# Second-layer weights in pieces of two depth blocks by all columns, instead of whole depth by 256 columns

## The chip, the cores and the metric

The kernel runs on one core of one Trainium2 chip. The metric is the device time of one execution in microseconds (us). A measurement is the median of several runs.

## What is computed

A two-layer decoder trunk on 256 positions of width 1024, in float32. Layer 0 is a gated short convolution, layer 1 a forgetting attention whose key, value and forget gates come from the residual stream. Both layers also attend to 256 memory rows, and both end in a PEER layer: 128 table rows per position are chosen out of 16,384, and gathered from two tables.

```python
for layer in range(2):
    if layer == 1:
        hs = rmsnorm(x, g_kv)
        zkv = hs @ w_kv                     # keys 768, values 768, forget gates 12 columns
    h = rmsnorm(x, g_mix[layer])
    mkv = rmsnorm(mem, g_mem[layer]) @ w_mem_kv[layer]
    if layer == 0:
        z = h @ w_in_a[0]                   # u, c, b (768 each), memory queries 256
        y_main = b_gate * causal_dwconv(c_gate * u, conv_w[0])
    else:
        z = h @ w_in_b[0]                   # queries 768, memory queries 256
        y_main = fox_attention(qf, k_sh, v_sh, logf_sh)
    x = x + concatenate([y_main, mem_attention(qm, mk, mv)]) @ w_out[layer]
    # peer: q = xn @ w_q; top 16 x 16 keys per head, 8 heads; then for each position
    #   a = xn . u_tab[idx];  w = softmax(score) * gelu(a);  out = sum(w * v_tab[idx])
    x = x + peer(rmsnorm(x, g_ffn[layer]), peer_wq[layer], ...)
return rmsnorm(x, g_final)
```

## The kernel before

**Phases and groups.** The positions are cut into two chunks of 128, one position per partition. A phase is one chunk's PEER layer: phases 0 and 1 are layer 0 of chunks 0 and 1, phases 2 and 3 are layer 1 (chunk c has phase c + 2). A phase has 16 groups, and a group handles 8 of the 128 table rows of each position. Each of the 8 slots of a group takes one gather of 128 u rows and one of 128 v rows, 4 KB per row, into `u_ring` and `v_ring` (8 slots each). GpSimd issues them (`fetch`, line 519; `group`, line 536): the v gather of slot s waits until the sums of the group before have read that slot, the u gather of the next group until VectorE's dot product of that slot is done. VectorE makes the dots (line 1010) and folds in one v slot itself (line 1037); ScalarE makes gelu, gates and seven diagonal matrices (lines 596 to 611); TensorE adds the other seven v slots into PSUM `acc` (line 795).

**Side steps.** The rest of the network is cut into steps, and `make_schedule` (line 71) writes out by hand in which group each is done: `SIDE[phase, group]`. TensorE does the side steps of a group ahead of that group's sums; VectorE and ScalarE do them after that group's dots and diagonals. A route step (`("route", ph, h)`) projects one head's 256 query columns, transposes them, scores them against the keys on TensorE, and gives VectorE the choice of the top rows. VectorE runs that part (line 1258) spread between the dots of the next group, in order. The attention, key, value, query and output steps of layer 1 of chunk c lie in groups 0 to 9 of phase c + 1: keys in group 1, values and forget gates in 2, queries in 3, attention in 4 to 8, output in 8.

**Weights.** SyncE loads all weights in pieces of 1 MB in the order of their first use (line 468). A piece is the whole depth (8 blocks of 128 rows) by 256 columns, so each run in memory is 1 KB. Eight pieces of the first layer have places of their own inside the gather rings (`HELD`), one lies in `kv_buf` (`GUEST`), all others take turns in `w_ring` with `NW` = 5 slots. A load into a slot waits for the last tile that uses the piece five places earlier (line 480), and SyncE keeps its order. The `out` and `q` pieces of layer 0 are loaded once for both chunks, those of layer 1 once for each chunk.

**Tiles.** A projection's result is a PSUM tile in one of four banks (six at the start). Keys and queries are made with the weights as the stationary side (`columns_out`, line 768: two blocks of 128 columns in a tile), values, outputs and routes with the activations stationary (`tokens_out`, line 777: 256 columns in a tile). `take` (line 747) waits for the bank, `piece_landed` (line 415) for the piece, `filled` and `emptied` (lines 396 and 399) for a tile. The first output tile of a chunk waits for all parts of `yT` (line 868).

Of the kernel before, what the change touches and what calls it, by code (L numbers as in the profile page):

```python
# [32 lines left out]
P = 128  # L33
# [8 lines left out]
CONV_K = 3  # L42
PC = 256
NPAIR = D // P
HEADS = 8
# [25 lines left out]
def make_schedule():  # L71

    def attn(ph, *ks):
        return [("attn", ph, k) for k in ks]

    def out(ph, *cols):
        return [("out", ph, i) for i in cols]

    def conv(c, *parts):
        return [("in", c, int(p[1]), p[0]) for p in parts]

    def rms(*step):
        return ("rms", step)


    chunk0 = [*conv(0, "b0"), ("mem_k", 0), *conv(0, "u1"), ("in_q",), ("mem_v", 0), *attn(0, 0), *conv(0, "c1"),
              *attn(0, 1), *conv(0, "b1"), *attn(0, 2), *conv(0, "u2"), *attn(0, 3), *conv(0, "c2"), ("keys", 0),
              *conv(0, "b2"), *out(0, 0, 1, 2, 3)]  # L90
# [118 lines left out]

def piece_of(tile):  # L210

    kind = tile[0]
    if kind == "mT":
        return "mem", tile[1]
    if kind == "key":
        return "keys", tile[1]
    if kind == "out":
        return (kind, 0, tile[2]) if tile[1] < 2 else tile
    if kind == "q":
        return (kind, 0, tile[2]) if tile[1] < 2 else tile  # L220
    if kind in ("u", "c", "b"):
        return kind, tile[2]
    return tile if kind in ("mk", "mv", "qm", "k", "v", "qf") else None

# [3 lines left out]
for _t in TILES:  # L228
    if piece_of(_t):
        LAST_USE[piece_of(_t)] = _t  # L230

# [5 lines left out]
for _n in range(NW, len(PIECES)):  # L237
    assert TILE[LAST_USE[PIECES[_n - NW]]] < min(TILE[t] for t in TILES if piece_of(t) == PIECES[_n])


def trunk(nc, x, mem, g_mix, w_in_a, conv_w, w_in_b, w_out, g_mem, w_mem_kv, g_kv, w_kv, b_f, g_ffn,
# [5 lines left out]
    def weight_source(key):  # L247
# [4 lines left out]
        if kind == "keys":  # L252
            return peer_keys[key[1]].rearrange("h t n d -> n (h t) d")
        w, col = {
            "mk": lambda: (w_mem_kv[key[1]], 0),
# [4 lines left out]
            "qm": lambda: (w_in_a[0], 3 * CONV),  # L260
            "k": lambda: (w_kv, PC * key[2]),
            "v": lambda: (w_kv, CONV + PC * key[2]),
            "qf": lambda: (w_in_b[0], PC * key[2]),
            "out": lambda: (w_out[key[1] // 2], PC * key[2]),
            "q": lambda: (peer_wq[key[1] // 2], PC * key[2]),
# [3 lines left out]
    with ExitStack() as ctx:  # L269
# [186 lines left out]
        def _(sp):  # L456
# [11 lines left out]
            for key in LAST_USE:  # L468
                src = weight_source(key)
                dst = piece(key).rearrange("p (a b) -> p a b", a=src.shape[1])  # L470
                if key in HELD:
# [9 lines left out]
                sp.dma_start(dst, src).then_inc(w_landed[n % NW], 16)  # L481
                if key == ("out", 0, 0):
                    load_gain_row(g_ffn[0])
# [104 lines left out]
        def _(act):  # L588
# [32 lines left out]
            def side(step):  # L621
# [24 lines left out]
                elif kind == "k":  # L646
                    _, c, i = step
                    if c == 0 and i == 0:
                        filled(act, ("mv", 1))
                    copy_tile(step, kT[:, 2 * i:2 * i + 2, P * c:P * c + P],  # L650
                              bank(step)[:, 0:2 * P].rearrange("p (a b) -> p a b", a=2))
                elif kind == "v":
                    _, c, i = step
                    copy_tile(step, vals[:, c, PC * i:PC * i + PC], bank(step)[:, 0:PC])
                elif kind == "forget":
                    act.wait_ge(fabs_made, step[1] + 1)
                    act.activation(fz[:, 2, :], fz[:, 1, :], ACT.Exp, scale=-1.0).then_inc(fexp_made, 1)
                elif kind == "qf":
                    _, c, i = step
                    if c == 1:  # L660
                        filled(act, ("lg", 2, NPAIR - 1))
                    copy_tile(step, qT[:, 2 * i:2 * i + 2, :],
                              bank(step)[:, 0:2 * P].rearrange("p (a b) -> p a b", a=2))
                elif kind == "attn":
# [30 lines left out]
                    if k >= 2:  # L695
                        key = ("y", ph, k - 2)
                        if ph >= 2 and k == 2:
                            filled(act, ("out", ph - 2, 3))
                        copy_tile(key, yT[:, pairs[k - 2], P * c:P * c + P], bank(key)[:, 0:P])
# [44 lines left out]
        def _(pe):  # L744
# [32 lines left out]
            def tokens_out(key, src):  # L777
# [4 lines left out]
                done(project(t[:, 0:PC], src, lambda k: w[:, k, :]))  # L782

            def transposes(key, blocks):
                t = take(key)
# [14 lines left out]
            def side(step):  # L800
# [44 lines left out]
                elif kind == "k":  # L845
                    if step[2] == 0:
                        for i in range(2):
                            emptied(pe, ("nT", step[1], i))
                    columns_out(step, lambda k: hT[:, k, 0:P], P)
                elif kind == "v":  # L850
                    tokens_out(step, lambda k: hT[:, k, 0:P])
                elif kind == "forget":
# [9 lines left out]
                elif kind == "qf":  # L862
                    columns_out(step, lambda k: hT[:, k, P:2 * P], P)
# [37 lines left out]
            def attention(ph, k):  # L901

                c, pairs = ph % 2, attention_pairs(ph)
                if k == 0:
                    if ph < 2:
                        emptied(pe, ("qm",))
                    else:
                        for i in range(4):
                            emptied(pe, ("qf", c, i))
                        for i in range(3):  # L910
                            emptied(pe, ("k", c, i))
# [69 lines left out]
        def _(dve):  # L981
# [102 lines left out]
            def start_norm(step):  # L1084
# [11 lines left out]
                elif kind == "ffn":  # L1096
                    ph = step[1]
                    if ph >= 2:
                        filled(dve, ("fT", ph - 2, 1))
                    for i in range(4):  # L1100
                        emptied(dve, ("out", ph, i))
# [7 lines left out]
            def side(step):  # L1109
# [22 lines left out]
                elif kind == "norm":  # L1132
                    c = step[1]
                    filled(dve, ("qf", 0, 3) if c else ("b", 1, NB // 2 - 1))
                    for i in range(2):
# [11 lines left out]
                elif kind == "out":  # L1147
                    _, ph, i = step
                    filled(dve, step)
                    part = xres[:, ph % 2, PC * i:PC * i + PC]  # L1150
                    empties(dve.tensor_tensor(part, part, bank(step)[:, 0:PC], ALU.add), step)
                elif kind == "ffn":
# [249 lines left out]
```

## Time and profile before

| | |
|---|---|
| Runs | 1630.38 us median of 3 (1630.02 to 1630.99) |
| Profiled execution | span of 1628.2 us from the first to the last instruction; its own total is not given apart from the span |
| TensorE busy | 1330.9 us, 82% |
| VectorE busy | 1073.0 us, 66% |
| ScalarE busy | 468.4 us, 29% |
| GpSimd busy | 1013.0 us, 62% |
| DMA | 619.20 MB, mean 380 GB/s |
| Mean granted TensorE clock | 0.907 of full speed |

A busy share is an average over stages that have different limits. The page cuts the span into 40 slices, each of 40.7 us. The first three slices are the start (first layer up to the first routes), and the gathers run from 117 us to the end. On the DMA lines q0 is GpSimd's queue of gathers, and q1 SyncE's queue of weights and other plain loads. Every gather is reported with some very small packets beside its 4 KB ones.

### The profile page before, as it was taken

The page shows a single profiled execution, that of the slowest core. Times are in us where ns is not written, and L with a number is a line of the kernel's source. Part 1 is how long each engine was busy: PE and PEld are TensorE (multiplying, and loading weights), DVE is VectorE, ACT ScalarE, POOL GpSimd, SP SyncE. Part 2 cuts the span into 40 slices and gives each one's busy share as a digit, 9 for nine tenths or more (in the row PEclk, how much of TensorE's full clock was granted, in tenths as well). Part 3 has the DMA queues.
Part 4 walks back from the last instruction along what each step waited for, and adds up shares of the span by engine and source line. Part 5 has one row for each costly group of instructions (what it writes and reads, how often), then busy time and mean ns, then how long its engine had stood idle before and what let it go on. Part 6 is the DMA issues. An engine that isn't in the chain of part 4 may idle for free.

```text
span 1628.2 us, 17186 instructions
## 1 busy us (share of the span) xinstructions
PE 1330.9 (82%) x4558; PEld 768.0 (47%) x4558; DVE 1073.0 (66%) x2529; ACT 468.4 (29%) x1427; POOL 1013.0 (62%) x1099
## 2 busy tenths in 40 slices
PE   7999789888885899887877789989868877777775
PEld 7887544444552564354444366545434432222222
DVE  4248689988775445638778835674878985555555
ACT  0203343333332222433233222451333321111112
POOL 0006677777547656667666654675776777777764
PEclk9999898999998999899888899999999988888887
DMA  9519999999999999999999999999999999999997
GB/s 336 185 53 372 397 399 409 405 404 405 379 391 378 396 393 394 409 405 390 401 401 403 401 376 384 397 397 393 400 403 409 409 411 409 410 409 410 410 409 272
DMA packets 224232, 619.20 MB, mean 380 GB/s; under 512 B 18914, under 2 KB 90652, under 8 KB 224156
## 3 DMA queue, kind: packets, MB, share of 16 engines
q0 software_dynamic: 147456, 536.94, 83.7%
q1 hardware_dynamic: 76699, 81.36, 15.0%
q8 instruction: 35, 0.57, 0.1%
q14 instruction: 42, 0.34, 0.1%
HBM read 617.17 MB, written 1.05 MB: 380 GB/s over the span
## 4 chain that ended last, share of the span: by engine, by line
PE 36%; DMA 22%; POOL 13%; issue 12%; DVE 9%; ACT 5%; POOLq 0%; SPq 0%; DVEq 0%; ACTq 0%
DMA u_ring<-in_peer_u_dram,idx_now 20%; PE acc L795 18%; PE tile L765 13%; POOL u_ring L520 7%; POOL v_ring L520 7%; DVE u_ring L1010 4%; ACT diag L610 2%; DMA v_ring<-in_peer_v_dram,idx_now 2%; ACT gelus L604 2%; PE xf L765 1%; PE tile L897 1%; PE tile L924 1%; PE tile L892 1%; PE tile L928 0%; PE tile L787 0%
## 5 line engine op out<-in xcount | busy, mean ns | idle before, releaser
L795 PE MATMUL acc<-v_ring,diag 128*128 128x512 f32 x1780 | 852.9, 637 | 118.5 <-ACT diag L610 74.0
L1010 DVE CUSTOM_DVE_ANT_0 u_ring<-u_ring,xf 128x1024 f32<-128x1024 f32 x512 | 613.2, 1216 | 270.2 <-DMA u_ring<-in_peer_u_dram,idx_now 267.2
L520 POOL DMA_INDIRECT v_ring<-in_peer_v_dram,idx_now x512 | 495.4, 968 | 294.5 <-issue 121.9
L795 PEld LDWEIGHTS acc<-v_ring,diag 128*128 128x128 f32 x1780 | 359.9, 207 | 581.3 <-issue 565.9
L520 POOL DMA_INDIRECT u_ring<-in_peer_u_dram,idx_now x512 | 503.3, 983 | 173.4 <-issue 126.5
L596 ACT ACTIVATE gelus<-dots 128x8 f32<-128x8 f32 x64 | 13.4, 209 | 515.4 <-DVE dots L1010 515.4
L610 ACT ACTIVATE diag<-ident,gelus 128x128 f32<-128x128 f32 x448 | 137.8, 388 | 2.1
L765 PE MATMUL tile<-w_ring,fT 128*128 128x256 f32 x480 | 110.4, 384 | 6.4 <-DVE fT L1159 6.4
L765 PEld LDWEIGHTS tile<-w_ring,fT 128*128 128x128 f32 x480 | 92.0, 192 | 30.3 <-issue 12.0
L604 ACT ACTIVATE gelus<-gelus,gates 128x1 f32<-128x1 f32 x512 | 102.1, 281 | 4.9 <-ACT gelus L596 3.3
L714 ACT ACTIVATE gexp<-best,gstat 128x16 f32<-128x16 f32 x32 | 9.8, 307 | 306.9 <-DVE best L1300 306.9
L892 PE MATMUL tile<-ident,q_rows 128*128 128x128 f32 x64 | 17.7, 368 | 86.7 <-ACT q_rows L704 86.7
L1037 DVE SCALAR_TENSOR_TENSOR xres<-v_ring,gelus,xres 128x1024 f32<-128x1024 f32 x63 | 80.9, 1284 | 8.7 <-issue 8.7
L765 PE MATMUL tile<-hT,w_ring 128*128 128x128 f32 (+1 forms) x544 | 69.7, 293 | 15.1 <-issue 13.1
L765 PEld LDWEIGHTS tile<-hT,w_ring 128*128 128x128 f32 x544 | 68.0, 203 | 17.7 <-issue 14.5
L570 POOL COPY idx_now<-idx_all 128x8 uint32<-128x8 uint32 x1 | 0.2, 187 | 114.2 <-DVE idx_all L1329 114.2
L596 ACT ACT_TABLE_LOAD x45 | 57.7, 1283 | 0.8
L765 PE MATMUL tile<-w_ring,yT 128*128 128x256 f32 x224 | 51.1, 389 | 5.8 <-ACT yT L619 4.9
L892 PEld LDWEIGHTS tile<-ident,q_rows 128*128 128x128 f32 x64 | 7.7, 169 | 99.6 <-ACT q_rows L704 99.6
L765 PEld LDWEIGHTS tile<-w_ring,yT 128*128 128x128 f32 x224 | 43.3, 195 | 12.5 <-issue 6.4
L897 PE MATMUL tile<-keysT,pq 128*128 128x128 f32 x128 | 32.4, 396 | 15.1 <-ACT pq L706 15.1
L1010 DVE DVE_READ_ACCUMULATOR2_ANT dots<- 128x1 f32 x512 | 42.1, 82 | 0.0
(170 smaller groups left out, 1043.0 us busy)
## 6 DMA issues: line engine op xcount, KB each, us to landing
w_ring<-in_peer_wq_dram SPq DMA_DIRECT2D x23, 1024.0 KB, 16.5
w_ring<-in_w_out_dram SPq DMA_DIRECT2D x12, 1024.0 KB, 16.8
w_ring<-in_w_kv_dram SPq DMA_DIRECT2D x12, 1024.0 KB, 16.9
u_ring<-in_peer_u_dram,idx_now POOLq DMA_INDIRECT x512, 11.5
v_ring<-in_peer_v_dram,idx_now POOLq DMA_INDIRECT x512, 11.0
w_ring<-in_w_in_b_dram SPq DMA_DIRECT2D x8, 1024.0 KB, 16.5
u_ring<-in_w_in_a_dram SPq DMA_DIRECT2D x4, 1024.0 KB, 12.2
w_ring<-in_w_mem_kv_dram SPq DMA_DIRECT2D x4, 1024.0 KB, 15.4
```

The source lines that it names most:

```text
L520: pool.indirect_dma_start(ring[:, s, :], None, rows_[:, :], bass.IndirectOffsetOnAxis(idx_now[:, column + s:column + s + 1], 0), element_o ...
L596: act.activation(gelus[:, par * G:par * G + G], dots[:, par * G:par * G + G], ACT.Gelu)\
L604: act.activation(gelus[:, par * G + s:par * G + s + 1], gelus[:, par * G + s:par * G + s + 1], ACT.Copy, scale=gate[:, col + s:col + s + 1 ...
L610: act.activation(diag[:, par * G + s, :], ident[:, :], ACT.Copy, scale=gelus[:, par * G + s:par * G + s + 1]).then_inc(diag_made, 1)
L714: act.activation(gexp[:, :], best[:, :], ACT.Exp, bias=gstat[:, 0:1], accum_out=gstat[:, 1:2]).then_inc(gexp_made, 1)
L765: ins = pe.matmul(out_ap, lhs(k), rhs(k), start=(k == 0), stop=(k == KD - 1))
L795: ins = pe.matmul(acc[:, 512 * n:512 * n + 512], diag[:, par * G + s, :], v_ring[:, s, 512 * n:512 * n + 512], start=(first and s == 0), s ...
L892: ins = pe.transpose(t[:, P * a:P * a + P], q_rows[:, P * a:P * a + P], ident[:, :])
L897: ins = pe.matmul(t[:, NKEY * a:NKEY * a + NKEY], pq[:, a, :], keysT[:, 2 * h + a, :], start=True, stop=True)
L924: ins = pe.matmul(t[:, hh, 0:width], q, keys, start=True, stop=not fox)
L1010: dve.tensor_tensor_reduce(u_ring[:, s, :], u_ring[:, s, :], xf[:, :], 1.0, 0.0, ALU.mult, ALU.add, dots[:, par * G + s:par * G + s + 1])\
L1037: dve.scalar_tensor_tensor(out=row, in0=v_ring[:, s, :], scalar=gelus[:, par * G + s:par * G + s + 1], in1=row, op0=ALU.mult, op1=ALU.add) ...
```

## The change

The second layer's key, value and query weights, and the output weights of both layers, are cut the other way: a piece holds two depth blocks (256 rows) by all wanted columns. Key and value pieces have 768 columns, 3 KB rows and 0.79 MB; query and output pieces have 1024 columns, 4 KB rows and 1.05 MB. Four pieces make one matrix, and every tile reads all four (`pieces_of`). The tiles become wider to fit: keys in tiles of 4 and 2 blocks, queries in two tiles of 4 blocks, values in two tiles of 384 columns, outputs in two of 512. Value and output tiles wait for their pieces two blocks at a time, and the first output tile waits for the parts of `yT` as it comes to them; key and query tiles wait for all four pieces at once. The step `("route", 0, 2)` moves from the head of the side steps of group (0, 1) to their end. The pieces of routes, memory and the other first-layer weights stay as they are.

```diff
+VC = CONV // 2
+OC = D // 2
+K_BLOCKS = [4, 2]
...
-    side[0, 0] += [*conv(1, "c2", "b2"), ("route", 0, 1), *out(1, 0, 1)]
-    side[0, 1] += [*out(1, 2, 3), rms("ffn", 1)]
+    side[0, 0] += [*conv(1, "c2", "b2"), ("route", 0, 1), *out(1, 0)]
+    side[0, 1] += [*out(1, 1), rms("ffn", 1)]
...
-    side[0, 1][0:0] = [("route", 0, 2)]
+    side[0, 1] += [("route", 0, 2)]
...
-        mix[1] += [("norm", c), ("k", c, 0), ("k", c, 1), ("k", c, 2)]
-        mix[2] += [("v", c, 0), ("v", c, 1), ("v", c, 2), ("forget", c)]
-        mix[3] += [("qf", c, 0), ("qf", c, 1), ("qf", c, 2), ("qf", c, 3)]
+        mix[1] += [("norm", c), ("k", c, 0), ("k", c, 1)]
+        mix[2] += [("v", c, 0), ("v", c, 1), ("forget", c)]
+        mix[3] += [("qf", c, 0), ("qf", c, 1)]
...
-        mix[8] += attn(ph, 9) + out(ph, 0, 1, 2, 3) + [rms("ffn", ph)]
+        mix[8] += attn(ph, 9) + out(ph, 0, 1) + [rms("ffn", ph)]
...
-def piece_of(tile):
+def pieces_of(tile):
...
+    if kind in ("k", "v", "qf"):
+        return [("w" + kind, tile[1], kk) for kk in range(KD // 2)]
     if kind == "out":
-        return (kind, 0, tile[2]) if tile[1] < 2 else tile
+        return [("wout", max(tile[1] - 1, 0), kk) for kk in range(KD // 2)]
...
+        if kind in ("wk", "wv", "wqf", "wout"):
+            w, col, width = {
+                "wk": lambda: (w_kv, 0, CONV),
+                "wv": lambda: (w_kv, CONV, CONV),
+                "wqf": lambda: (w_in_b[0], 0, D),
+                "wout": lambda: (w_out[min(key[1], 1)], 0, D),
+            }[kind]()
+            k = 2 * key[2]
+            return w.rearrange("(k p) n -> p k n", p=P)[:, k:k + 2, col:col + width]
...
+            def blocks_out(key, src, blocks, width):
+
+                t = take(key)
+                for at in pieces_of(key):
+                    piece_landed(pe, at)
+                for a, b in enumerate(blocks):
+                    ins = project(t[:, P * a:P * a + P], lambda k: rows_of(key, k, P * b, width), src)
+                done(ins)
+
+            def tokens_wide(key, src, cols, width, order=range(KD), ready=None):
+
+                t = take(key)
+                for n, k in enumerate(order):
+                    if n % 2 == 0:
+                        piece_landed(pe, pieces_of(key)[k // 2])
+                        if ready:
+                            ready(k // 2)
+                    ins = pe.matmul(t[:, 0:len(cols)], src(k), rows_of(key, k, None, width)[:, cols.start:cols.stop],
+                                    start=(n == 0), stop=(n == KD - 1))
+                done(ins)
...
-                    if i == 0:
-                        for k in range(len(attention_pairs(ph))):
-                            emptied(pe, ("y", ph, k))
-                        if ph < 2:
-                            for j in range(NB // 2):
-                                emptied(pe, ("b", ph, j))
-                    tokens_out(step, lambda k: yT[:, k, P * (ph % 2):P * (ph % 2) + P])
+                    order = [6, 7, 0, 1, 2, 3, 4, 5] if ph < 2 else range(KD)
...
+                    tokens_wide(step, lambda k: yT[:, k, P * (ph % 2):P * (ph % 2) + P],
+                                range(OC * i, OC * i + OC), D, order, mixed if i == 0 else None)
```

## Rows read from the trace of the kernel before

**Rows 1.** The page: DMA share and rate in 40 slices, and the weight queue.
```profile
DMA  9519999999999999999999999999999999999997
GB/s 336 185 53 372 397 399 409 405 404 405 379 391 378 396 393 394 409 405 390 401 401 403 401 376 384 397 397 393 400 403 409 409 411 409 410 409 410 410 409 272
...
q1 hardware_dynamic: 76699, 81.36, 15.0%
```

**Rows 2.** Busy time by stretch; last columns: TensorE clock, DMA share, GB/s.
```profile
551.00:596.00 45.00, 41.06 (x158) 26.28 (x157) 18.80 (x44) 11.16 (x36) 21.27 (x24) 0.92 1.05 386
650.00:700.00 50.00, 36.95 (x108) 17.03 (x107) 32.32 (x64) 25.42 (x83) 35.47 (x37) 0.87 1.03 409
```

**Rows 3.** Waits over the span: waiting, releaser, us in total, times, longest.
```profile
DVE u_ring L1010 <- DMA u_ring<-in_peer_u_dram,idx_now: 267.2, 218, 5.7
```

**Rows 4.** DMA queues, 551 to 596 us: packets, MB, share of 16 engines.
```profile
q1 hardware_dynamic: 6001, 6.06, 40.8%
```

**Rows 5.** DMA queues, 156 to 158 us.
```profile
q1 hardware_dynamic: 696, 0.70, 110.1%
```

**Rows 6.** DMA queues, 186 to 192 us.
```profile
q0 software_dynamic: 339, 1.26, 52.9%
q1 hardware_dynamic: 349, 1.17, 49.1%
```

**Rows 7.** Timeline of TensorE, 163 to 201 us: start, duration, instructions, idle before.
```profile
163.81 3.62 PE L765 MATMUL tile<-w_ring,fT 128*128 128x256 f32 x16
167.92 0.44 PE L892 MATMUL tile<-ident,q_rows 128*128 128x128 f32 x2 [0.49 <-ACT q_rows L704]
...
169.38 7.07 PE L765 MATMUL tile<-w_ring,yT 128*128 128x256 f32 x32
176.28 12.18 PE L795 MATMUL acc<-v_ring,diag 128*128 128x512 f32 x28
...
200.17 0.69 PE L892 MATMUL tile<-ident,q_rows 128*128 128x128 f32 x2 [7.37 <-ACT q_rows L704]
```

**Rows 8.** DMA queues at 150 to 152 us, and the weight issue at 148.
```profile
q1 hardware_dynamic: 1, 0.00, 0.1%
...
w_ring<-in_peer_wq_dram SPq DMA_DIRECT2D x1, 1024.0 KB, 9.9
```

**Rows 9.** Timeline of GpSimd, 153 to 206 us.
```profile
153.48 0.19 POOL L550 COPY idx_now<-idx_all 128x8 uint32<-128x8 uint32 x1 [3.67 <-DVE idx_all L1329]
153.95 0.96 POOL L520 DMA_INDIRECT v_ring<-in_peer_v_dram,idx_now  x1 [0.28 <-PE acc L795]
...
178.44 0.96 POOL L520 DMA_INDIRECT v_ring<-in_peer_v_dram,idx_now  x1 [4.00 <-PE acc L795]
...
206.03 0.96 POOL L520 DMA_INDIRECT v_ring<-in_peer_v_dram,idx_now  x1 [4.91 <-PE acc L795]
```

**Rows 10.** Timeline of VectorE: the first instruction of route (0, 2).
```profile
182.57 0.49 DVE L1266 MAX8 topv<-tile 128x8 f32<-128x128 f32 x2
```

**Rows 11.** Timeline of TensorE, 555 to 612 us.
```profile
555.19 12.18 PE L795 MATMUL acc<-v_ring,diag 128*128 128x512 f32 x28
567.21 10.52 PE L765 MATMUL tile<-w_ring,hT 128*128 128x256 f32 x48
...
597.82 14.45 PE L765 MATMUL tile<-hT,w_ring 128*128 128x128 f32 x128
```

**Rows 12.** Timeline of GpSimd: the gathers that end its two stalls.
```profile
557.89 0.96 POOL L520 DMA_INDIRECT v_ring<-in_peer_v_dram,idx_now  x1 [7.18 <-DVE dots L1010]
...
957.29 0.96 POOL L520 DMA_INDIRECT v_ring<-in_peer_v_dram,idx_now  x1 [12.71 <-PE acc L795]
```

**Rows 13.** DMA queues, 950 to 958 us.
```profile
q1 hardware_dynamic: 2374, 2.40, 91.9%
```

**Rows 14.** Timeline of TensorE: the output steps of chunks 0 and 1, layer 1.
```profile
716.61 14.05 PE L765 MATMUL tile<-w_ring,yT 128*128 128x256 f32 x64 [1.35 <-ACT yT L619]
...
1115.49 15.74 PE L765 MATMUL tile<-w_ring,yT 128*128 128x256 f32 x64 [3.59 <-ACT yT L619]
```

More of the change, by code:

```diff
@@ L89, in make_schedule @@
               *attn(0, 1), *conv(0, "b1"), *attn(0, 2), *conv(0, "u2"), *attn(0, 3), *conv(0, "c2"), ("keys", 0),
-              *conv(0, "b2"), *out(0, 0, 1, 2, 3)]
+              *conv(0, "b2"), *out(0, 0, 1)]
     chunk1 = [*conv(1, "b0", "u1", "c1"), *attn(1, 0), *conv(1, "b1"), *attn(1, 1), *conv(1, "u2"), *attn(1, 2, 3)]
@@ L207, with piece_of @@
 LAST_ROUTE = {ph: [r for r in ROUTES if r[0] == ph][-1] for ph in range(PHASES)}
-def piece_of(tile):
+def pieces_of(tile):
     kind = tile[0]
     if kind == "mT":
-        return "mem", tile[1]
+        return [("mem", tile[1])]
     if kind == "key":
-        return "keys", tile[1]
+        return [("keys", tile[1])]
+    if kind in ("k", "v", "qf"):
+        return [("w" + kind, tile[1], kk) for kk in range(KD // 2)]
     if kind == "out":
-        return (kind, 0, tile[2]) if tile[1] < 2 else tile
+        return [("wout", max(tile[1] - 1, 0), kk) for kk in range(KD // 2)]
     if kind == "q":
-        return (kind, 0, tile[2]) if tile[1] < 2 else tile
+        return [(kind, 0, tile[2]) if tile[1] < 2 else tile]
     if kind in ("u", "c", "b"):
-        return kind, tile[2]
-    return tile if kind in ("mk", "mv", "qm", "k", "v", "qf") else None
+        return [(kind, tile[2])]
+    return [tile] if kind in ("mk", "mv", "qm") else []
+def piece_of(tile):
+    return pieces_of(tile)[0]
 LAST_USE = {}
 for _t in TILES:
-    if piece_of(_t):
-        LAST_USE[piece_of(_t)] = _t
+    for _p in pieces_of(_t):
+        LAST_USE[_p] = _t
 HELD = [("c", 0), ("b", 0), ("u", 1), ("c", 1), ("b", 1), ("u", 2), ("c", 2), ("b", 2)]
@@ L237 @@
 for _n in range(NW, len(PIECES)):
-    assert TILE[LAST_USE[PIECES[_n - NW]]] < min(TILE[t] for t in TILES if piece_of(t) == PIECES[_n])
+    assert TILE[LAST_USE[PIECES[_n - NW]]] < min(TILE[t] for t in TILES if PIECES[_n] in pieces_of(t))
 def trunk(nc, x, mem, g_mix, w_in_a, conv_w, w_in_b, w_out, g_mem, w_mem_kv, g_kv, w_kv, b_f, g_ffn,
@@ L260, in weight_source @@
             "qm": lambda: (w_in_a[0], 3 * CONV),
[L261 to L264, printed above, removed]
             "q": lambda: (peer_wq[key[1] // 2], PC * key[2]),
@@ L469, in _ @@
                 src = weight_source(key)
-                dst = piece(key).rearrange("p (a b) -> p a b", a=src.shape[1])
+                dst = piece(key)[:, 0:src.shape[1] * src.shape[2]].rearrange("p (a b) -> p a b", a=src.shape[1])
                 if key in HELD:
@@ L481, in _ @@
                 sp.dma_start(dst, src).then_inc(w_landed[n % NW], 16)
-                if key == ("out", 0, 0):
+                if key == ("wout", 0, 0):
                     load_gain_row(g_ffn[0])
@@ L661, in side @@
                         filled(act, ("lg", 2, NPAIR - 1))
-                    copy_tile(step, qT[:, 2 * i:2 * i + 2, :],
-                              bank(step)[:, 0:2 * P].rearrange("p (a b) -> p a b", a=2))
+                    copy_tile(step, qT[:, 4 * i:4 * i + 4, :],
+                              bank(step)[:, :].rearrange("p (a b) -> p a b", a=4))
                 elif kind == "attn":
@@ L697, in side @@
                         if ph >= 2 and k == 2:
-                            filled(act, ("out", ph - 2, 3))
+                            filled(act, ("out", ph - 2, 1))
                         copy_tile(key, yT[:, pairs[k - 2], P * c:P * c + P], bank(key)[:, 0:P])
@@ L782, in tokens_out, with rows_of @@
                 done(project(t[:, 0:PC], src, lambda k: w[:, k, :]))
+            def rows_of(key, k, first, width):
+                at = pieces_of(key)[k // 2]
+                w = piece(at)[:, 0:2 * width].rearrange("p (k n) -> p k n", k=2)
+                return w[:, k % 2, first:first + P] if first is not None else w[:, k % 2, :]
+            def blocks_out(key, src, blocks, width):
[15 more added lines that the diff above has]
+                done(ins)
             def transposes(key, blocks):
@@ L848, in side @@
                             emptied(pe, ("nT", step[1], i))
-                    columns_out(step, lambda k: hT[:, k, 0:P], P)
+                    i = step[2]
+                    blocks_out(step, lambda k: hT[:, k, 0:P], range(4 * i, 4 * i + K_BLOCKS[i]), CONV)
                 elif kind == "v":
-                    tokens_out(step, lambda k: hT[:, k, 0:P])
+                    i = step[2]
+                    tokens_wide(step, lambda k: hT[:, k, 0:P], range(VC * i, VC * i + VC), CONV)
                 elif kind == "forget":
@@ L862, in side @@
                 elif kind == "qf":
-                    columns_out(step, lambda k: hT[:, k, P:2 * P], P)
+                    blocks_out(step, lambda k: hT[:, k, P:2 * P], range(4 * step[2], 4 * step[2] + 4), D)
                 elif kind == "attn":
@@ L907, in attention @@
                     else:
-                        for i in range(4):
+                        for i in range(2):
                             emptied(pe, ("qf", c, i))
-                        for i in range(3):
                             emptied(pe, ("k", c, i))
@@ L1099, in start_norm @@
                         filled(dve, ("fT", ph - 2, 1))
-                    for i in range(4):
+                    for i in range(2):
                         emptied(dve, ("out", ph, i))
@@ L1133, in side @@
                     c = step[1]
[L1134 removed]
+                    filled(dve, ("qf", 0, 1) if c else ("b", 1, NB // 2 - 1))
                     for i in range(2):
@@ L1149, in side @@
                     filled(dve, step)
-                    part = xres[:, ph % 2, PC * i:PC * i + PC]
-                    empties(dve.tensor_tensor(part, part, bank(step)[:, 0:PC], ALU.add), step)
+                    part = xres[:, ph % 2, OC * i:OC * i + OC]
+                    empties(dve.tensor_tensor(part, part, bank(step)[:, 0:OC], ALU.add), step)
                 elif kind == "ffn":
```

13 lines of the change are left out of this document (10 added, 3 removed).

## The prediction

> **What bounds the kernel now.** Read the page first: the DMA engines are over nine tenths busy in every slice but the first three, at 370 to 411 GB/s [rows 1]. A stretch of gathers alone moves 409 GB/s at a share of 1.03, the full rate [rows 2]. The waits agree: VectorE waits 267.2 us for rows of the u table, 218 times, never over 5.7 us [rows 3], a steady drip as behind a full queue. So from the first gather to the end the time is the DMA work divided by its rate, plus whatever idle DMA time a stall makes. The change touches both.
>
> **The work, smaller.** With both queues loaded, 551 to 596 us, the rate is 386 GB/s against 409 [rows 2]: 45 us x 23/409 = 2.53 us lost, on 6.06 MB of weights [rows 4], that is 0.44 us for a piece of 1.05 MB. The packets say why: weights alone, 696 packets of 1 KB took 110.1% of 16 engines for 2 us, 50.6 ns each, 50 us of engine time a MB [rows 5]. In the one stretch where the weight queue holds 4 KB rows (mem and the gain row, 186 to 192 us) it moved 1.17 MB in 49.1% of 96 us, 40.3 us a MB, and the gathers beside it 1.26 MB in 52.9%, the same [rows 6]. So 4 KB rows should give the 0.44 us back, and 3 KB rows, by a fixed cost per packet, 8/9 of it, 0.39 us. Twelve MB of key and value weights and sixteen of query and output weights in the two streaming chunks: 12 x 0.39 + 16 x 0.44 = 11.7 us. Bounds: nothing, and 28 x 0.53 = 14.8 us by the engine shares instead of the rate. I take the rate, since in a mix the share reads 1.05 and part of it is overlap [rows 2]. The first layer's output weights load before any gather: nothing.
>
> Against this stands a rule of the Trainium skill (DMA: Bandwidth & Descriptors, Specifications): line rate needs only transfers of 512 B or more, by which 1 KB rows lose nothing and this term is zero. By that rule, the 50 and 40 us a MB should have been equal; the trace disagrees.
>
> **Work on the engines.** Columns and passes stay; the matmuls are wider and fewer. Two 256-column output tiles take 7.07 us [rows 7], and a group of seven 2 x 512-column sums 12.18 us, 0.87 us for 512 columns against 0.44 for 256: no gain. Copies and adds of twice the width lie beside other work: nothing. The output step of the first chunk no longer waits for the last gate product before its first matmul: -0.6 us (0 to -0.9), as that start is a chain.
>
> **The moved step, route 2 of the first chunk.** All four first-layer output pieces are now last used by output tile 1 of chunk 1, in group 1. The query piece (0, 2) takes the slot of the first, so it can load only then; and TensorE's very next step is the route that needs it. Before, it was issued at 148.54 and landed 9.9 us later [rows 8], under the first group's sums. Now TensorE starts at 163.81 with the output tile (7.07 us) and is done at 170.9 [rows 7]. The issue's first packet came 3.3 us after it (one packet by 152 [rows 8]). From there it shares with the gathers one packet for one: 349 to 339 packets in rows 6. The 16 gathers of a group (v and u of eight slots) are issued from 153.95 until GpSimd's next stall, which ends with 4.00 us of waiting at 178.44 [rows 9]; each is 0.524 MB, 1.285 us at 409 GB/s, and beside the weights the last is through at about 180.3; the piece is then half in, and lands near 183. TensorE stands 12 us. It comes back at the low clock, as after the 7.37 us wait at 200.17, when two transposes took 0.69 instead of 0.44 us [rows 7]; the projection of 3.62 us takes some 6, two small copies and products 2.2: scores at 191.2. Queued behind are the sums of group 1: 191.2 instead of 176.28. Behind them waits GpSimd for a v slot: 193.3 instead of 178.44 [rows 9], 14.9 us late. VectorE waits inside group 2 for the scores, 191.2 instead of 182.57 [rows 10], so the diagonals of group 2 and its sums are 8 us late.
>
> The DMA engines meanwhile: (1) in the gap of 3.67 us where GpSimd waited for indices, the early loads used to run alone, no gather packet between 156 and 158 [rows 5, 9]; now nothing is there: 3.8 us idle. (2) After 180.3 the remaining 4.1 MB of query pieces, gain row and mem last until about 192.7, and gathers issued at 193.3 show packets some 4.5 us later (after the one at 153.95 the weights still had all engines until 158 [rows 5]): 5.1 us idle. Together 8.9; I take 7.5, since group 3 of the gathers restarts at 213.4 instead of 206.03. Bounds: 0 (in 116 to 225 us VectorE waits for no gather, so it may be hidden) and 14.9, the whole delay.
>
> **The pieces wanted together.** Five slots, four per step: value pieces 1 to 3 and query piece 0 are issued only when the last key tile is done, 12.0 us before the value step; the next four when the values are done at 577.7, with a group's sums between. Before, they trickled out tile by tile. TensorE has no gap here: sums from 555.19, values 567.21, query columns 597.82, no wait ahead of any [rows 11]. With 3 and 4 KB rows against gathers of 4 KB they get 43 to 50% of the engines instead of 25%: the three value pieces, 2.36 MB, get the whole engines while the gathers are dry (1.5 MB by 562) and 176 GB/s after, landed by 569 (the last is wanted near 571, since each pair is waited for by itself); three query pieces, 3.15 MB from 580.9 at half of 409 GB/s, by 597.3 (wanted 597.8). I cost that at 0, cover 0.5 to 2 us; without cover see below.
>
> What they no longer do is fill gaps. GpSimd stands 7.18 and 12.71 us before 557.89 and 957.29 [rows 12]. In the second stall the weights had 91.9% of the engines for 8 us [rows 13]; now the first is issued when the keys are done, 954.7, GpSimd's restart less the 2.6 us that the first slot's sums and its own start take. With no weight queued the gathers dry up at 556.1 and 950.6; the first new packets come near 557.4 (an empty queue answers in some 2 us) and 956.7. Idle: 1.3 (0 to 2.4) and 6.1 less 1.0 that was idle already, 5.1 (3 to 7.4). At the output steps the next query pieces come after the last tile instead of tile by tile: about 2.5 us lost each, of which the waits of 1.35 and 3.59 us ahead of the output step [rows 14] give back most, as three of four weight pairs run before the last y is wanted: 1.0 and 0.6 (0 to 3 each). Sum of the gaps: +8.0 (3 to 15).
>
> **Sum.** -11.7 - 0.6 + 7.5 + 8.0 = +3.2 us on a profiled span of 1628.2: 1631.4. The profiled run's own total is not given; the median of the runs, 1630.38, stands 2.2 us above the span, kept for what lies around it: 1633.6, and rounding up for the throttled restarts, **1634.0**. A measurement of this kernel can tell about 0.2%, 3.3 us, from no change.
>
> **Rivals.**
> 1. *Faster: the stalls are absorbed.* The route's wait delays a stage in which no dot waits for a gather, and the queue stays fed by the four waiting loads; only the 3.8 us of the first gap are lost and half the others. -11.7 - 0.6 + 3.8 + 3 = -5.5: **1625**. For it: the missing waits in 116 to 225 us, and TensorE's 7.37 us wait at 200 that can shrink. Against: the DMA share is at its full value there. It decides if the gathers of group 3 start before about 209 us. Chance 0.22.
> 2. *Both signs cancel in TensorE's stretch.* In 555 to 612 TensorE is never idle for long, so cheaper packets gain less and gaps cost less: within 3 us, **1630**. Against: VectorE's waits for u go on in that stretch. Chance 0.10.
> 3. *Pieces late.* If larger rows get no larger share, 3.1 MB of query pieces need until about 602 and values until 573: 4 + 2 us of TensorE waiting per chunk, 12 in all, the DMA working through part of it: +10, **1644**. Against: equal packet counts in rows 6. Chance 0.13.
> 4. *No saving.* Row length costs nothing: -0.6 + 7.5 + 8.0 = +14.9, **1645**. Against: rows 5 and 6. Chance 0.05. The skill's 512 B rule, named above, would have it so.
>
> **How the numbers follow.** The forecast's case has 0.50 and spans 1626 to 1640 by its terms' bounds: 0.27 of it slower by over 0.2%, 0.21 within, 0.02 faster. Rival 1 is faster; rival 2 gives 0.08 within and 0.02 faster; rivals 3 and 4 are slower. Faster 0.26, within 0.29, slower 0.45. The likeliest case's own range is 1628 to 1639; the range for 8 in 10, reaching into rivals 1 and 3, is 1622 to 1645.
>
> **What would show it.** Right: the weight queue's 76,699 packets [rows 1] fewer by about 23,500 (32 pieces of 1,024 become 36 of 256), and over 395 GB/s where 386 was; a TensorE idle of 10 to 14 us near 171 to 183 ahead of the query projection, and GpSimd's v gather near 193; a DMA share well below 1 at 152 to 158 and near 951 to 956. Wrong: no TensorE gap near 171; a rate unchanged at 386 GB/s; waits of TensorE inside the value or query steps of the second layer; the second layer's groups ending over 6 us nearer to or farther from the start stage than these terms say.

## The result, and the profile after

The changed kernel takes 1639.51 us (median of 4, 1638.75 to 1643.03) against 1630.20 us before: the ratio is 1.0058, with an interval of 1.0046 to 1.0071. It is slower by 9.3 us. The profiled run is the slowest of the four (1643.03 us, span 1641.2 us), so shares of its span are taken of 1641.2 us, and the sizes of terms come from timed runs.

The page of the changed kernel, with the lines that answer to [rows 1]:

```profile
DMA  9529999999997999999999989999999999999996
GB/s 335 186 61 346 347 405 409 402 405 406 394 390 302 386 410 405 409 409 379 401 408 408 408 351 409 405 389 396 395 403 409 409 410 409 410 410 410 410 408 250
...
q1 hardware_dynamic: 53211, 81.36, 14.0%
```

The weight queue has 23,488 packets fewer, as said, moves the same bytes, and takes 14.0% of 16 engines: 229.8 us instead of 15.0% of 1628.2, 244.2 us. So the DMA engines were given less to do, some 14 us less by their share, and yet the end is later. The rates say where: 346 and 347 GB/s in the fourth and fifth slices, 302 in the 13th (492 to 533 us, a slice being 41 us), 351 in the 24th (944 to 985 us).

First the start. The timeline of TensorE, against [rows 7]:

```profile
162.85 7.03 PE L823 MATMUL tile<-w_ring,yT 128*128 128x512 f32 x16
182.33 5.17 PE L781 MATMUL tile<-w_ring,fT 128*128 128x256 f32 x16 [12.45 <-DMA w_ring<-in_peer_wq_dram]
187.97 0.44 PE L941 MATMUL tile<-ident,q_rows 128*128 128x128 f32 x2 [0.47 <-ACT q_rows L720]
188.88 0.71 PE L946 MATMUL tile<-keysT,pq 128*128 128x128 f32 x4 [0.47 <-ACT pq L722]
189.43 12.18 PE L838 MATMUL acc<-v_ring,diag 128*128 128x512 f32 x28
```

The wait for the query piece stands ahead of route (0, 2), 12.45 us long; the projection then takes 5.17 us instead of 3.62. The granted clock was 0.50 from 178 to 182 us, at the end of the wait, and 0.59 from 182 to 186, so most of the projection ran at the lower of TensorE's two levels, 1.2 GHz. The sums of group 1 start at 189.43 instead of 176.28. GpSimd's timeline shows who is queued behind that, and the stalls at the turn of phases and ahead of the value and query steps, against [rows 9, 12]:

```profile
191.59 0.96 POOL L535 DMA_INDIRECT v_ring<-in_peer_v_dram,idx_now  x1 [16.65 <-PE acc L838]
...
500.13 0.19 POOL L565 COPY idx_now<-idx_all 128x8 uint32<-128x8 uint32 x1 [19.03 <-DVE idx_all L1377]
...
567.99 0.96 POOL L535 DMA_INDIRECT v_ring<-in_peer_v_dram,idx_now  x1 [6.42 <-PE acc L838]
...
963.85 0.96 POOL L535 DMA_INDIRECT v_ring<-in_peer_v_dram,idx_now  x1 [12.05 <-PE acc L838]
```

Before the change the stall at the turn was this:

```profile
490.19 0.19 POOL L550 COPY idx_now<-idx_all 128x8 uint32<-128x8 uint32 x1 [14.54 <-DVE idx_all L1329]
```

Busy time by stretch in the changed kernel (columns as in [rows 2]; the last three are clock, DMA share and GB/s):

```profile
154.00:158.00 4.00, 4.00 (x11) 1.74 (x10) 4.00 (x9) 0.00 (x0) 2.56 (x3) 1.00 0.65 177
192.00:194.00 2.00, 2.00 (x6) 0.95 (x5) 1.97 (x6) 0.00 (x0) 1.49 (x2) 1.00 0.38 51
480.00:490.00 10.00, 10.00 (x24) 4.37 (x23) 6.38 (x21) 2.89 (x5) 0.93 (x1) 1.00 1.03 406
492.00:504.00 12.00, 0.00 (x0) 0.00 (x0) 7.38 (x14) 3.95 (x16) 3.03 (x4) 0.66 0.24 82
956.00:964.00 8.00, 8.00 (x55) 6.49 (x54) 4.89 (x7) 2.48 (x10) 0.15 (x1) 1.00 0.34 107
```

The same two stretches at the turn, before the change:

```profile
480.00:490.00 10.00, 6.71 (x16) 2.66 (x14) 7.71 (x18) 4.18 (x15) 0.00 (x0) 1.00 1.08 363
492.00:504.00 12.00, 7.09 (x12) 2.75 (x12) 3.31 (x5) 0.00 (x0) 9.19 (x10) 0.72 0.93 336
```

Three readings. The two idle spots of the start are where they were forecast, near 155 and 193 us. The one near 956 is there too. And there is one that the prediction did not name: from 492 to 504 us the DMA share is 0.24, 9 us of idle engines. There GpSimd waits for VectorE's indices of the next phase, TensorE has nothing, and only weights could use the time. Before, four pieces of 1 MB were loaded over this turn, and 3.2 MB of them moved after 480 us; now it is four pieces of 0.79 MB, and only 0.4 MB of them is left at 492 us. This is how the two queues shared the engines from 478 to 490 us:

```profile
q0 software_dynamic: 742, 2.71, 56.2%
q1 hardware_dynamic: 750, 2.18, 46.7%
```

And before the change, from 474 to 480 us:

```profile
q0 software_dynamic: 511, 1.85, 78.5%
q1 hardware_dynamic: 515, 0.52, 25.2%
```

Packet for packet again (742 to 750, and 511 to 515), but a packet of weights is 3 KB now: the weights take 46.7% of the engines instead of 25.2% while the gathers still want them, and are used up when the gathers run dry.

The same share delays the gathers, and the end of the stall hangs on them. VectorE works out the last indices of the next phase in small steps between the dots of the last group, in order; the step that releases GpSimd comes 3.8 us after the start of the last dot, in both kernels. The last u gather and its dot, before and after the change:

```profile
474.72 0.94 POOL L520 DMA_INDIRECT u_ring<-in_peer_u_dram,idx_now  x1 [0.30 <-issue]
486.17 1.22 DVE L1010 CUSTOM_DVE_ANT_0 u_ring<-u_ring,xf 128x1024 f32<-128x1024 f32 x1 [1.24 <-DMA u_ring<-in_peer_u_dram,idx_now]
...
480.16 0.93 POOL L535 DMA_INDIRECT u_ring<-in_peer_u_dram,idx_now  x1 [0.30 <-issue]
496.11 1.22 DVE L1058 CUSTOM_DVE_ANT_0 u_ring<-u_ring,xf 128x1024 f32<-128x1024 f32 x1 [2.02 <-DMA u_ring<-in_peer_u_dram,idx_now]
```

From the issue to the dot it is 11.45 us before and 15.95 after, 4.5 us more, and GpSimd's stall grows by the same 4.5 us, from 14.54 to 19.03.

### The profile page after: what moved, and what is told of

The parts are those of the page before. It is cut to its first block, busy times and chain, and to the rows that moved or that the text cites. A ratio compares the mean times of both kernels' runs of the same rounds, so it can differ in the third digit from the quotient of the medians.

```text
span 1641.2 us, 16840 instructions
## 1 busy us (share of the span) xinstructions
PE 1347.8 (82%) x4398; PEld 744.9 (45%) x4398; DVE 1072.7 (65%) x2521; ACT 467.0 (28%) x1419; POOL 1018.0 (62%) x1099
## 3 DMA queue, kind: packets, MB, share of 16 engines
HBM read 617.17 MB, written 1.05 MB: 377 GB/s over the span
## 4 chain that ended last, share of the span: by engine, by line
PE 35%; DMA 24%; issue 12%; POOL 12%; DVE 9%; ACT 6%; POOLq 0%; SPq 0%; ACTq 0%; DVEq 0%
DMA u_ring<-in_peer_u_dram,idx_now 21%; PE acc L838 19%; PE tile L781 8%; POOL v_ring L535 6%; POOL u_ring L535 6%; PE tile L823 5%; DVE u_ring L1058 4%; DMA v_ring<-in_peer_v_dram,idx_now 2%; ACT diag L625 2%; ACT gelus L619 2%; DMA w_ring<-in_peer_wq_dram 1%; PE tile L946 1%; PE tile L830 1%; PE tile L972 1%; PE tile L941 0%
## 5 line engine op out<-in xcount | busy, mean ns | idle before, releaser
L838 PE MATMUL acc<-v_ring,diag 128*128 128x512 f32 x1780 | 871.0, 649 | 112.8 <-ACT diag L625 68.3
L535 POOL DMA_INDIRECT v_ring<-in_peer_v_dram,idx_now x512 | 502.0, 980 | 301.5 <-PE acc L838 127.7
L838 PEld LDWEIGHTS acc<-v_ring,diag 128*128 128x128 f32 x1780 | 367.2, 211 | 587.5 <-issue 573.6
L781 PE MATMUL tile<-w_ring,fT 128*128 128x256 f32 x480 | 113.1, 390 | 19.4 <-DMA w_ring<-in_peer_wq_dram 12.4
L823 PE MATMUL tile<-w_ring,yT 128*128 128x512 f32 x128 | 56.0, 594 | 0.0
L1314 DVE MAX8 topv<-tile 128x8 f32<-128x128 f32 x64 | 15.8, 289 | 47.1 <-PE tile L946 47.0
```

The costliest lines, as they stand in the source:

```text
L535: pool.indirect_dma_start(ring[:, s, :], None, rows_[:, :], bass.IndirectOffsetOnAxis(idx_now[:, column + s:column + s + 1], 0), element_o ...
L781: ins = pe.matmul(out_ap, lhs(k), rhs(k), start=(k == 0), stop=(k == KD - 1))
L823: ins = pe.matmul(t[:, 0:len(cols)], src(k), rows_of(key, k, None, width)[:, cols.start:cols.stop], start=(n == 0), stop=(n == KD - 1))
L838: ins = pe.matmul(acc[:, 512 * n:512 * n + 512], diag[:, par * G + s, :], v_ring[:, s, 512 * n:512 * n + 512], start=(first and s == 0), s ...
```

## The experiments

Every version computes the whole result; none leaves work out. Each ratio is against the kernel before on the same chip. Differences between two variants are taken between their ratios, times 1630 us.

**1. The first-layer part taken back, and the first-layer part alone.**

```diff
-    side[0, 0] += [*conv(1, "c2", "b2"), ("route", 0, 1), *out(1, 0)]
-    side[0, 1] += [*out(1, 1), rms("ffn", 1)]
+    side[0, 0] += [*conv(1, "c2", "b2"), ("route", 0, 1), *out(1, 0, 1)]
+    side[0, 1] += [*out(1, 2, 3), rms("ffn", 1)]
...
-    side[0, 1] += [("route", 0, 2)]
+    side[0, 1][0:0] = [("route", 0, 2)]
...
-        return [("wout", max(tile[1] - 1, 0), kk) for kk in range(KD // 2)]
+        if tile[1] >= 2:
+            return [("wout", max(tile[1] - 1, 0), kk) for kk in range(KD // 2)]
+        return [("out", 0, tile[2]) if tile[1] < 2 else tile]
```

> The changed kernel with its first-layer part taken back: layer 0's output weights again in four pieces of 256 columns, route (0, 2) again at the head of group (0, 1), all of layer 1 as changed. Theory A (TensorE's 12.45 us wait for the query piece costs the time of some 7 us, measured as GpSimd's group marks 6.2 to 7.0 us late from the sixth group on): about 1632.5 us, 7 us faster than the changed kernel, and 2 to 3 us slower than before. Rival (that lag is absorbed later, the loss is all in the second layer's gaps): 1639, no change.

Measured: 1632.91 us (median of 11), ratio 1.0014 (1.0005 to 1.0023). That is 0.0044 below the changed kernel: 7.2 us.

The second kernel keeps the first-layer lines of the change and takes back those of layer 1 (its pieces, tile widths and step lists are the old ones):

```diff
     if kind in ("k", "v", "qf"):
-        return [("w" + kind, tile[1], kk) for kk in range(KD // 2)]
+        return [tile]
...
+        if tile[1] < 2:
+            return [("wout", max(tile[1] - 1, 0), kk) for kk in range(KD // 2)]
+        return [("out", 0, tile[2]) if tile[1] < 2 else tile]
```

> Only the first-layer part of the change: layer 0's output weights in pieces of two depth blocks and the moved route, all of layer 1 as before. Theory A: 1630.2 + 7 = 1637 us, with TensorE idle for 12 to 13 us near 182 us. Rival: 1630 to 1632, the wait is there and is made up before the end.

Measured: 1637.29 us (median of 5), ratio 1.0049 (1.0036 to 1.0063), 8.0 us. Its timeline of TensorE has the wait:

```profile
181.24 6.71 PE L787 MATMUL tile<-w_ring,fT 128*128 128x256 f32 x16 [12.05 <-DMA w_ring<-in_peer_wq_dram]
```

Both agree: this part costs 7 to 8 us, and no regain later in the run can be seen, though no dot product waited for a gather in that stage (116 to 225 us). The rivals that had it absorbed fall. The two kernels switch the wide output pieces, the wider output tiles and the moved step together; that the wait makes the cost is read from the timeline. What is left for all of layer 1 is 2.3 us of loss (0.8 to 3.7), where the prediction had a gain of 3.7.

**2. Rows of 1 KB in the same pieces.** The pieces, their order, the slots and the waits stay; only the transfers are cut.

```diff
-                sp.dma_start(dst, src).then_inc(w_landed[n % NW], 16)
+                if parts_of(key) == 1:
+                    sp.dma_start(dst, src).then_inc(w_landed[n % NW], 16)
+                else:
+                    for at in range(0, PC * parts_of(key), PC):
+                        sp.dma_start(dst[:, :, at:at + PC], src[:, :, at:at + PC]).then_inc(w_landed[n % NW], 16)
```

> The changed kernel, each wide piece of weights loaded by three or four transfers of 256 columns, so in runs of 1 KB, the pieces, their order and their release unchanged. Theory B (long rows save 0.39 to 0.44 us a piece of DMA time, 11.7 us, but take half the engines and so are gone when the gathers run dry): DMA idle time falls by 7 or more at the turn from phase 0 to 1 near 496 us, the rate where both queues are busy falls from 408 to 386 GB/s, and value and query pieces come 3 to 6 us too late for TensorE, per chunk: 1643 to 1652 us. Rival (row length is worth nothing): 1631 to 1638, since the turn is filled again and nothing is lost.

Measured: 1653.34 us (median of 5), ratio 1.0134 (1.0113 to 1.0155), 12.4 us above the changed kernel. At the turn, while the weights load, the rate falls to 386 GB/s, from 406:

```profile
478.00:492.00 14.00, 12.39 (x39) 6.08 (x37) 12.59 (x42) 5.14 (x8) 3.28 (x4) 1.00 1.05 386
```

And TensorE waits inside the value steps of both chunks (its timeline):

```profile
582.71 9.22 PE L840 MATMUL tile<-w_ring,hT 128*128 128x384 f32 x20 [5.37 <-DMA w_ring<-in_w_kv_dram]
...
983.21 8.41 PE L840 MATMUL tile<-w_ring,hT 128*128 128x384 f32 x20 [2.28 <-DMA w_ring<-in_w_kv_dram]
```

That stretch holds some microseconds of weights alone; from 580 to 590 us, where the gathers run throughout, it is 395 GB/s, against 409 from 572 to 580 us in the changed kernel. TensorE waits for the values alone, not for the queries. So the value pieces, which are wanted together, are on time only because their long packets get half of the engines: the cover on which the prediction put a cost of nothing is real. The 12.4 us are several effects together: 7.7 us of waits and the packets' price, less what is won back at the turn, where GpSimd's stall is 12.59 us instead of 19.03. How they divide is not shown, since the profiled run (1647.71 us) is 5.6 us faster than the median; the next run takes the turn by itself.

**3. 1 KB rows at the turn alone.**

```diff
+def narrow_rows(key):
+
+    return key[:2] == ("wk", 0) or key == ("wv", 0, 0)
```

> The changed kernel, with 1 KB runs only for the five pieces that are waiting at the turn from phase 0 to 1 (chunk 0's four key pieces and its first value piece). Theory B: these pieces cost 2 us more DMA time, but last through the turn and win back most of its idle time (8 us more than before the change, between 480 and 505 us): 1634 to 1637 us. Rival (GpSimd waits at the turn for the indices, which long rows do not touch, so the idle time there moves but is not lost): 1640 to 1642.

Measured: 1635.87 us (median of 8), ratio 1.0029 (1.0019 to 1.004): 0.0029 below the changed kernel, 4.7 us. GpSimd's first copy after the turn comes 4.8 us later than before the change, where in the changed kernel it was 9.9 us later. The stretch by itself:

```profile
480.00:492.00 12.00, 11.22 (x27) 4.65 (x25) 8.76 (x27) 2.82 (x4) 0.68 (x1) 1.00 1.05 383
492.00:504.00 12.00, 3.38 (x4) 1.18 (x4) 5.55 (x11) 3.95 (x16) 6.78 (x8) 0.72 0.72 218
```

A share of 0.72 instead of 0.24: shorter rows, more DMA work, less time. Why GpSimd starts sooner, its own timeline and VectorE's say:

```profile
479.74 0.94 POOL L552 DMA_INDIRECT u_ring<-in_peer_u_dram,idx_now  x1 [0.30 <-issue]
495.02 0.19 POOL L582 COPY idx_now<-idx_all 128x8 uint32<-128x8 uint32 x1 [14.34 <-DVE idx_all L1394]
...
491.00 1.22 DVE L1075 CUSTOM_DVE_ANT_0 u_ring<-u_ring,xf 128x1024 f32<-128x1024 f32 x1 [1.30 <-DMA u_ring<-in_peer_u_dram,idx_now]
```

The weights take 24.1% of the engines from 480 to 486 us instead of 46.2%, the last u rows reach their dot 11.26 us after the issue instead of 15.95, and the stall is 14.34 us instead of 19.03: 4.7 us less, as much as the timed runs give. So the rival's condition does not hold, that long rows do not touch the indices. All the traces fit: where long rows stand at the turn the stall is 19.03 and 18.95 us (the changed kernel and the first of 1), in the other nine it is 12.6 to 15.8. This is the term that was missed.

**4. Both repairs.** Layer 0 as before, layer 1 as changed, 1 KB rows for the five pieces at the turn: the edits of 1 and 3 together.

> Both repairs together: layer 0 as before the change, layer 1 in wide pieces, 1 KB runs only for the five pieces that wait at the turn. If the first-layer wait (6.6 us by the run without it) and the turn (3.6 us by the run that mends it) are separate terms, 1639.5 - 6.6 - 3.6 = 1629.3 us, about the time before the change. If they overlap (the turn's gap depends on how late the start stage is), 1632.

Measured: 1628.00 us (median of 11), ratio 0.998 (0.9971 to 0.9988), 3.3 us faster than before the change. The terms add: 0.0058 - 0.0044 - 0.0029 = -0.0015, and -0.0020 was measured. Each term is thus measured twice: the turn by 4.7 us, and by 5.5 against the first kernel of 1 (1.0014 to 0.998); the first-layer part by 7.2 us, and by 8.0 against the kernel of 3 (1.0029 to 0.998).

**5. What a long row is worth alone.** First, only layer 1's output weights in wide pieces, the rest as before the change (key, value and query edits as in the second kernel of 1, layer 0 as in the first):

> Only layer 1's output weights in wide pieces, all else as before the change. Theory B: 8 pieces x 0.44 = 3.5 us saved, 1 to 2 us given back in the gaps behind the output steps: 1628 to 1629.5 us. Rival (long rows save nothing that reaches the end): 1630.5 to 1632.

Measured: 1631.33 us (median of 11), ratio 1.0000 (0.9992 to 1.0009). No gain can be seen, which is the rival's value, but it does not tell a saving of nothing from one that the gaps took back. The second run comes closer. It takes the version of 4 and cuts the rows of the output pieces, which have no deadline:

```diff
-    return key[:2] == ("wk", 0) or key == ("wv", 0, 0)
+    return key[:2] == ("wk", 0) or key == ("wv", 0, 0) or key[0] == "wout"
```

> The version with both repairs (1628.0 us), and layer 1's eight output pieces loaded in 1 KB runs too. They are not urgent: they land long before the output step. So this prices the row length alone. Theory B: 8 x 0.44 = 3.5 us slower, 1631.5 us. Rival (long rows save nothing that reaches the end, the gain of that version comes from elsewhere): 1628.

Measured: 1630.67 us (median of 11), ratio 0.9995 (0.9986 to 1.0004), 0.0015 above the version of 4: 2.4 us for 8 pieces, 0.30 us each. The intervals of the two just overlap, so the size is uncertain by about as much as itself. Its middle lies between nothing and the 0.44 us that the rates gave. Short rows also give these pieces a smaller share beside the gathers, so even this run does not price the packets alone.

**6. Giving pieces back sooner.** From the version of 4. The two value tiles of a step, and the two output tiles, are made together, depth pair by depth pair, and SyncE waits for a count of used pieces:

```diff
+            def tokens_together(keys, src, cols, width, ready=None):
+
+                ts = [take(key) for key in keys]
+                for kk, at in enumerate(pieces_of(keys[0])):
+                    piece_landed(pe, at)
...
+                    for i, t in enumerate(ts):
+                        for k in (2 * kk, 2 * kk + 1):
+                            ins = pe.matmul(t[:, 0:cols], src(k),
+                                            rows_of(keys[i], k, None, width)[:, cols * i:cols * i + cols],
+                                            start=(k == 0), stop=(k == KD - 1), skip_group_check=True)
...
+                    if kk < KD // 2 - 1:
+                        used(ins, at)
...
-                if n >= NW:
+                if n >= NW and PIECES[n - NW] in RELEASED:
+                    sp.wait_ge(w_used, RELEASED.index(PIECES[n - NW]) + 1)
+                elif n >= NW:
                     filled(sp, LAST_USE[PIECES[n - NW]])
```

> As the run with both repairs, and value and output tiles of a step are made together, depth pair by depth pair, so that each piece but the last is given back as soon as it is used. If the gaps at the output steps matter, 1 to 2 us less than that run: about 1628 us. If not, the same time as it.

Measured: 1626.83 us (median of 12), ratio 0.9978 (0.997 to 0.9987). Not to be told from the version of 4 (0.998). Then keys and queries too, with the same loop over blocks (`blocks_together`):

> The same for key and query tiles too, so that the next pieces are issued from the middle of the key step, 3 to 9 us sooner, ahead of GpSimd's stalls of 6.4 and 12.05 us. Theory B (the idle DMA time at 566 and at 956 to 963 us is lost time): 3 to 5 us less than with values and outputs alone, about 1624 us. Rival (pieces come too late or TensorE is the bound there): no gain, 1628.

Measured: 1628.45 us (median of 11), ratio 0.9981 (0.9972 to 0.999): no gain, though the idle DMA time ahead of the value step is gone. Stretches with values and outputs alone:

```profile
940.00:950.00 10.00, 10.00 (x76) 8.80 (x76) 6.08 (x9) 2.08 (x8) 0.00 (x0) 0.99 0.45 157
```

And with keys and queries too:

```profile
940.00:950.00 10.00, 10.00 (x77) 8.83 (x77) 3.69 (x6) 0.98 (x2) 0.00 (x0) 1.00 1.03 404
...
1020.00:1050.00 30.00, 27.75 (x86) 15.25 (x84) 19.05 (x36) 13.50 (x41) 15.00 (x16) 0.83 0.94 348
```

With values and outputs alone the later stretch was this:

```profile
1020.00:1050.00 30.00, 27.76 (x108) 15.39 (x106) 20.89 (x39) 11.96 (x38) 17.91 (x21) 1.00 1.03 403
```

From 157 to 404 GB/s in the key step, and nothing comes of it: TensorE is busy for all 10 us in both, the sums after it start at 947.75 and 947.88 us, and GpSimd's next restarts are at 950.44 and 950.57, 981.30 and 981.29 us. Idle DMA time in this stretch was not lost time. Later the share is 0.94 instead of 1.03, and GpSimd's stall there 9.55 us instead of 4.59. Whether the early loading causes this is not shown: the version with only the output pieces wide, which gives nothing back early, has a stall of 9.60 us in the same place.

## Why the prediction was right, and by how much it was off

The forecast was slower, 1634.0 us in 1622 to 1645; measured 1639.5, so the sign and the range held. The forecast difference to the median before was 3.6 us, and the measured one 9.3. The first-layer part carries the sign: it was forecast at 6.9 us and measured at 7.2 to 8.0. For layer 1 the sign was wrong, a gain of 3.7 us forecast and a loss of 2.3 measured.

**The moved route: right, step by step.** Forecast: TensorE done with the output tile at 170.9, 12 us of standing, the piece landed near 183; measured: the output tile from 162.85 (0.9 us sooner, as the first output step was forecast 0.6 sooner), 12.45 us, the projection from 182.33. Projection 6 us: 5.17. Sums of group 1 at 191.2: 189.43. GpSimd at 193.3: 191.59. Cost 7.5 - 0.6 = 6.9 us: 7.2 us without that part, 8.0 with it alone. Taking idle DMA time as time, and not the wait itself (12.45) or GpSimd's delay (13 us), gave the size, and it held in a stage in which no dot product waited for DMA. How the idle time splits was off: by the shares of the profile the first spot (150 to 162 us) is idle for 2.8 us and the second (190 to 204) for 2.5, where 3.8 and 5.1 were forecast. By bytes the sum comes out: from 150 to 204 us 17.71 MB are moved instead of 21.29, which is 8.7 us at 409 GB/s, beside the forecast 8.9. Why the cost is the DMA time, when no dot waits for a gather there, is not shown.

**The pieces wanted together: right for TensorE, and the step that failed for everything beside it.** TensorE waits for none in the changed kernel (its only wait for a weight is the 12.45 us). With 1 KB rows it waits 7.7 us in the value steps, which is what rival 3 described. The equal packet counts [rows 6] were the row that decided it. But the prediction counted the larger share of the weights only as a help to the weights and costed it at 0. What it takes from the gathers has no term in the sum, and at the turn of phases it is the largest loss of layer 1, 4.7 us.

**The saving of 11.7 us: right in kind, its size not settled.** The queue's own share fell by some 14 us, and the rate at the turn is 406 GB/s with long rows and 386 with short ones. The upper bound was added up wrong: by the engine shares (50.6 ns for a 1 KB packet, 40.3 us a MB with long rows) a piece saves 0.53 us with 3 KB rows and 0.60 with 4 KB rows, 16.0 us in all and not 14.8; the bounds of the gaps add up to 15.8, not 15. Nothing else hangs on either. Cutting eight output pieces' rows cost 2.4 us where 3.5 were expected. With both repairs all of layer 1 gains 3.3 us; no run shows the 11.7.

**The gaps, 8.0 us: the wrong places.** They were chosen by looking for GpSimd's stalls in the key and output steps only. The longest stall after the gathers begin, 14.54 us at 490 us, was left out. Its releaser is VectorE's index chain, which the change does not edit; but the chain runs between dots that wait for u rows, and with long weight rows beside them those rows come 4.5 us later (11.45 against 15.95 us). Seen from the DMA engines it is the same loss: before, the weights still filled the stall, 363 GB/s at a share of 1.08 from 480 to 490 us; with long rows they are used up sooner, and 9 us stand idle. By the run with short rows there this costs 4.7 us. The gap that was priced highest instead, 5.1 us near 956 us, is there (a share of 0.75 from 950 to 970 us, 5 us), but costs nothing that can be measured: filling it gained nothing, and TensorE has no pause in that stretch, as rival 2 had it. So a sum of gaps not far from the right size (8.0 forecast, some 5 shown) stood on the wrong place, which is luck, and the rest of the error is the saving, of which less than 11.7 us reached the end.

**Row length and rate.** At the turn the same pieces were loaded at 386 GB/s in 1 KB rows and at 406 in 3 KB rows. That 512 B suffice for line rate (the Trainium skill, DMA: Bandwidth & Descriptors, Specifications) does not hold in this case for 1 KB rows against 3 KB ones.

Left open: why the executions of one version differ by several us (1625.67 to 1629.64 for the version of 4), and how the rest of the saving is divided among the pieces. A sixth weight slot, which might free route (0, 2) from its wait, was not tried.

## What to carry to other kernels

When a load is cut differently, three things change at once: what it costs, when its slot comes free, and how large a share it takes from its neighbours. Look for the neighbour on whose last transfer a stall hangs, and for the stall that the old, slower load used to fill. A piece that every tile of a matrix reads is held until the last tile: check which step needs the next piece right behind it. Cutting rows short on purpose, where a load is not urgent and the transfers beside it are, can be worth more than the bandwidth it wastes: the version with wide pieces in layer 1 only, and short rows at the turn, is 3.3 us faster than the kernel before. Giving pieces back early (3.6 us) can't be told from it.

## What was not expected of the hardware

Beside the gathers the two queues share the engines by packet count, not by bytes: 511 to 515 packets in 6 us with 1 KB rows of weights, 742 to 750 in 12 us with 3 KB, 339 to 349 in 6 us with 4 KB (the small packets of the gathers are among these). The prediction had read this; that it has a price was not expected. The row length of a load set its share against the other queue: 47% of the engines with 3 KB packets, where 1 KB packets had 25% beside gathers of 4 KB. At that share the last gathers before the turn took 4.5 us longer from issue to use. So some 14 us less engine time for the weights went together with a later end.
